# The order of three kinds of subtraction in VectorE's instruction stream, in a hybrid attention and convolution layer

## The reference

```
h    = x * (1 + scale(c)) + shift(c)                 # (2048, 1024), adaLN
proj = h @ w_in + b_in                               # (2048, 1024) @ (1024, 8704)
q, k, v, z_attn, u_x, g_b, g_c, z_conv, g_A, g_B = split(proj)
branch A: dilated sliding-window attention of 12 heads, groups mixed by their softmax denominators,
          (o * silu(z_attn)) @ w_proj_attn
branch B: (g_b * conv3(g_c * u_x) * silu(z_conv)) @ w_proj_conv
x_out = LayerNorm(alpha * x + gate(c) * ((sigmoid(g_A) * y_A + sigmoid(g_B) * y_B) @ w_out + b_out))
```

## Time and profile before

| | us |
|---|---|
| median of 3 runs | 1932.65 |
| lowest and highest | 1930.1, 1934.43 |
| the profiled execution, its time | 1930.85 |
| its span in the profile | 1929.0 |
| TensorE (PE) busy | 1910.6 |
| VectorE (DVE) busy | 1220.3 |
| ScalarE (ACT) busy | 856.1 |

### The profile page before, as it was taken

One profiled execution on the slowest core, in us unless ns is written; L12 is line 12 of the kernel. 1 busy time (PEld: TensorE's weight loads), 2 busy tenths in 40 slices (PEclk: granted clock), 3 DMA queues, 4 the chain that ended last, 5 costly groups with the idle time before them and its releaser, 6 DMA issues.

```text
span 1929.0 us, 25790 instructions
## 1 busy us (share of the span) xinstructions
PE 1910.6 (99%) x9101; PEld 1525.0 (79%) x9101; DVE 1220.3 (63%) x2164; ACT 856.1 (44%) x1506; POOL 199.9 (10%) x354
## 2 busy tenths in 40 slices
PE   8999999999999999999999999999999999999998
PEld 7888888877777777777777777777788888888886
DVE  6755744456666666665686666666656576646776
ACT  3644633344555454666675455544554410012221
POOL 0122111110000000111210000000011100000000
PEclk9999999999999999999999999999999999999999
DMA  9765833342222222364773223323256688884442
GB/s 328 263 204 189 283 99 119 94 112 82 78 83 83 80 79 83 102 206 152 259 265 92 82 83 90 94 86 94 81 150 177 215 242 246 235 269 137 140 144 96
DMA packets 307054, 289.05 MB, mean 150 GB/s; under 512 B 38548, under 2 KB 255760, under 8 KB 304240
## 3 DMA queue, kind: packets, MB, share of 16 engines
q1 hardware_dynamic: 280976, 200.06, 35.6%
q0 software_dynamic: 25952, 87.35, 12.5%
HBM read 198.97 MB, written 88.38 MB: 149 GB/s over the span
## 4 chain that ended last, share of the span: by engine, by line
PE 96%; DVE 2%; issue 1%; ACT 1%; DMA 0%; SPq 0%; DVEq 0%; ACTq 0%
PE acc L1144 22%; PE acc L1149 21%; PE acc L1152 21%; PE acc L1384 3%; PE acc L1319 3%; PE acc L1376 3%; PE acc L1315 3%; PE acc L1380 3%; PE acc L1311 3%; PE score L1221 3%; PE pt_o L1230 2%; PE xb L1253 2%; DVE ada_acc L1708 1%; PE xb L1256 1%; PE xb L1208 1%
## 5 line engine op out<-in xcount | busy, mean ns | idle before, releaser
L1144 PE MATMUL acc<-t_hi,w_hi 128*128 128x512 f32 x1848 | 511.8, 399 | 1.4 <-DVE room L1688 1.3
L1149 PE MATMUL acc<-t_lo,w_hi 128*128 128x512 f32 x1848 | 495.4, 390 | 0.0
L1152 PE MATMUL acc<-t_hi,w_lo 128*128 128x512 f32 x1848 | 495.0, 390 | 0.0
L1144 PEld LDWEIGHTS acc<-t_hi,w_hi 128*128 128x128 f32 x1848 | 336.0, 188 | 89.4 <-issue 20.1
L1149 PEld LDWEIGHTS acc<-t_lo,w_hi 128*128 128x128 f32 x1848 | 346.9, 188 | 74.6
L1152 PEld LDWEIGHTS acc<-t_hi,w_lo 128*128 128x128 f32 x1848 | 346.9, 188 | 74.0
L1688 DVE TENSOR_TENSOR room<-acc,part 128x512 f32<-128x512 f32 x198 | 136.6, 690 | 208.3 <-PE acc L1152 202.9
L1465 ACT ACTIVATE part<-acc,cols 128x512 f32<-128x512 f32 x198 | 136.1, 687 | 217.4 <-PE acc L1152 216.9
L1688 DVE TENSOR_TENSOR room<-room 128x512 f32<-128x512 f32 (+3 forms) x220 | 176.0, 804 | 73.5 <-ACT room L1495 27.4
L1688 DVE TENSOR_TENSOR w_lo<-w_raw,w_hi 128x512 fp32r<-128x512 f32 x272 | 184.2, 685 | 52.0 <-ACT w_hi L1448 51.3
L1448 ACT CAST w_hi<-w_raw 128x512 fp32r<-128x512 f32 x264 | 162.5, 616 | 93.0 <-PE acc L1152 89.7
(11 more groups left out here) (237 smaller groups left out, 2075.8 us busy)
## 6 DMA issues: line engine op xcount, KB each, us to landing
w_raw<-in_w_in SPq DMA_DIRECT2D x132, 512.0 KB, 5.1
gate_d<-room POOLq DMA_DIRECT2D x64, 256.0 KB, 2.8
w_raw<-gate_d SPq DMA_DIRECT2D x32, 512.0 KB, 5.5
qk_d<-room POOLq DMA_DIRECT2D x24, 512.0 KB, 4.2
room<-qk_d SPq DMA_DIRECT2D x192, 64.0 KB, 2.1
room<-in_x SPq DMA_DIRECT2D x32, 256.0 KB, 6.6
t_raw<-tr_d SPq DMA_DIRECT2D x8, 1024.0 KB, 8.4
conv_d<-room POOLq DMA_DIRECT2D x16, 512.0 KB, 2.9
```

The source lines that it names most:

```text
L1144: nc.tensor.matmul(to, w_hi[:, s, k], t_hi[:, p, k], start=(first and k == 0), stop=False, skip_group_check=True)
L1149: nc.tensor.matmul(to, w_hi[:, s, k], t_lo[:, p, k], start=False, stop=False, skip_group_check=True)
L1152: mm = nc.tensor.matmul(to, w_lo[:, s, k], t_hi[:, p, k], start=False, stop=(last and k == KH - 1), skip_group_check=True)
```

## The change

In VectorE's slot loop the block that calls `split_t` moves from behind `split_w` to ahead of `combine`. Nothing is added or removed; in the 14 slots that have a `split_t`, VectorE's order was `combine`, `split_w`, `split_t` and is `split_t`, `combine`, `split_w`.

```diff
                     if m - 2 in ATT_AT[2:]:
                         take_o(ATT_AT.index(m - 2) - 2)
+                    for ph in range(1, 3):
+                        for p in range(NP):
+                            if m == FIRST[ph] + T_LO_AT[p]:
+                                split_t(ph, p)
                     for n, when in enumerate((-4, -3, -2, 0)):
                         if (m - when) % NP == 0 and (m - when) // NP < NG:
                             combine((m - when) // NP, n)
                     if m + 3 < NS:
                         split_w(m + 3)
-                    for ph in range(1, 3):
-                        for p in range(NP):
-                            if m == FIRST[ph] + T_LO_AT[p]:
-                                split_t(ph, p)
```

## The result

The change makes the kernel slower: 1935.82 us (median of 20 runs, 1933.08 to 1938.87) against 1932.42 us (20 runs, 1928.37 to 1934.43). The ratio is 1.0020 with a 95% interval of 1.0013 to 1.0027, which is 3.9 us (2.5 to 5.2) on 1932.42; the two medians lie 3.40 us apart. Beside the experiments the same kernel was run again and gave 1.0031 (1.0019 to 1.0043).

A forecast was written before the change was run, and what follows sets the result against it. TensorE, busy 1910.6 of 1929.0 us, bounds the kernel, with VectorE setting its time at four products. VectorE's 2.80 us plus late loads of 0.95 and 0.4 give 4.15, so 1932.65 + 4.15 = 1936.8 us, range 1933.5 to 1940.0.

The forecast's parts named there:

- Where it counts: TensorE's late starts at products 62, 69, 300, 307: VectorE's sum of p = 4 already sets the time there.
- The four VectorE terms: VectorE, slots before products 62, 69, 300, 307: small subtractions leave a cast wait, delaying the sums 0.70, 0.71, 0.68, 0.71 us.
- SyncE in phase 1: Group 10's weights load 2.9 us later, delaying reloads 3 and 4, their casts and product 69 by 0.95 us.
- SyncE in phase 2: Group 44's late weight load makes reload 3 land at 996.0 instead of 993.1, its cast 0.4 us late.
- The sum: Whole kernel: 0.70 + 0.71 + 0.68 + 0.71 + 0.95 + 0.4 = 4.15 us slower.
- Loads that share the engines: SyncE's queue: weights, reloads 3 and 4 finish together, landing near 232.7 instead of 228.2; +13.6 us, 1946; chance 0.08.
- Hidden loads: Reloads 3 and 4 catch up, so only VectorE's reordering is paid: +2.8 us, 1935.4; chance 0.20.
- Not slower: t_lo of the same product ends the four stalls, so earlier `split_t(ph,6)` shortens them: 1931.0 to 1932.65; chance 0.14.

The follow-up runs named there:

- after_reload_first: Changed kernel, but SyncE issues the weight loads of groups 10 and 44 behind reload 3 of their phase; ratio to the kernel before 1.0010 (1.0001 to 1.0019).
- only_p5: Kernel before with only the `split_t` of reload 5 moved ahead (slots 66 and 304); ratio to the kernel before 1.0015 (1.0005 to 1.0025).
- w_t_combine: Changed kernel with `split_w` ahead of `split_t` again, `combine` still behind it; ratio to the kernel before 1.0000 (0.9991 to 1.0009).
- before_late_w: Kernel before, VectorE's order untouched, SyncE's weight loads of groups 10 and 44 held back for one more `split_w`; ratio 1.0028 (1.0019 to 1.0038).
- only_p1: Kernel before with only the `split_t` of reload 1 moved ahead (slots 59 and 297); ratio to the kernel before 1.0013 (1.0003 to 1.0022).
- after_but_one: Changed kernel with the `split_t` of reloads 3, 4 and 5 of phase 2 in their old place; ratio to the kernel before 1.0012 (1.0004 to 1.0021).
- after_again: The changed kernel run once more, unedited; ratio to the kernel before 1.0031 (1.0019 to 1.0043).
- only_p2_p6: Kernel before with only the `split_t` of reloads 2 and 6 moved ahead; ratio to the kernel before 0.9996 (0.9987 to 1.0005).

## Why the prediction was right, point by point

- *Where it counts.* Right: the four products 62, 69, 300 and 307, each waiting for VectorE's sum of p = 4.
- *The four VectorE terms,* 0.70, 0.71, 0.68, 0.71. Shown: 0.70, 0.70 (0.97 - 0.27, in after_reload_first and only_p5), 0.70, 0.72. The mechanism, small work pushed out of a wait, is shown by w_t_combine, which puts back one subtraction per wait and loses 0.4 us in all.
- *SyncE in phase 1,* 0.95. Right in mechanism (after_reload_first removes it, before_late_w enlarges it). Too large: 0.27 and 0.52 in the two profiles of the changed kernel, and 0.84 (only_p1) and 0.53 (after_but_one) in two more kernels with the late weight load. The step that was off is that a start 2.9 us later pushes every landing out by 2.9. In the profile after, reload 3 landed at 220.66 + 7.7 = 228.4 and reload 4 at 221.9 + 9.7 = 231.6; less the 0.50 us shift that is 2.6 and 2.2 us later than before. So the backlog did catch up, by 0.3 and 0.7 us, and by different amounts in different executions. The stated bounds, 0 to 1.6, hold all four. The prediction also tied this cost to `split_t(1,5)` starting on its cast; only_p1 shows it without that, through reload 4.
- *SyncE in phase 2,* 0.4. Mis-sized: nothing at product 307 in any profile of the changed order. Reload 3 landed at 989.9 + 7.9 = 997.8, which is 2.15 us later than before when the 2.55 us by which TensorE already ran late are taken off, not 2.9; its cast started at 998.19 and didn't wait.
- *The sum.* 4.15 forecast; the stalls grew by 3.1 and 3.3 us. The measured 3.9 (2.5 to 5.2) holds both. That it lies nearer the forecast than the stalls do is in part luck: the load terms were 1.1 and 0.8 us too large in sum, and the next point was missing.
- *What the forecast lacked.* A fall of the granted clock behind product 307. It came in all four profiles whose stall there was 2.0 us (the changed kernel twice, only_p5, after_reload_first) and in none of the nine with 1.56 us or less there, the kernel before among them. It adds about 1.7 us: 3.4 us at half speed. Whether it is part of the timed executions too stays open. By time: with it the changed kernel should be 4.8 to 5.0 us slower, and its two measurements, 3.9 (2.5 to 5.2) and 6.0 (3.7 to 8.3), allow it, the second better than 3.3 without it; after_reload_first should be 4.5 slower and measured 1.9 (0.2 to 3.7), where its stalls alone give 2.8. By clock: one such fall takes 0.0009 off the mean granted clock of an execution. Against the kernel before in the same session this mean was lower by 0.0013 in after_again (6 executions) and by 0.0007 in only_p5 (10), and not lower in after_reload_first (11) or after_but_one (11), with a standard error of 0.0002 to 0.0004 each (the clocks on record have three places). So it seems that most timed executions of the changed kernel have the fall and most of after_reload_first don't, though the one that was profiled has it. The comparison is weak, because the clock also falls in the first 50 us, for anything from 0 to 10.2 us in the thirteen profiled executions.
- *The rivals.* Loads that share the engines (+13.6) did not come: reload 3 landed 7.7 us after its issue, as before (7.5), and products 66 and 67 did not stall. Its price was also added up wrongly, since 10.8 us from 220.5 is 231.3 and not 232.7, and the 4.8 us late became 5.4 in the sum; the case lies far from the measurement either way. Hidden loads (+2.8) are true for phase 2 and not for phase 1. "Not slower" rested on t_lo of product 307 ending the stall; only_p2_p6 moves it 1.2 us earlier and changes nothing.

## What to carry to other kernels

When an engine runs a hand-written order and waits for another engine, the short work placed in front of that wait is free; put a step that is surely going to wait first, and the same work is paid in full wherever the engine has no idle time before its next deadline. Follow the moved work's own semaphores as well: here one late 0.6 us subtraction held back a weight load, behind it on the same queue four reloads, and behind these another engine's casts and sums. To find the better order, look for what stands in front of the operation that TensorE waits for and is needed later than it.

## What the runs showed of the hardware

Idle times of 1.85 to 1.88 us in front of product 307, where TensorE had had no longer idle time for over 990 us, were followed, in four profiles of four, by 3.4 us at 1.2 GHz in the middle of a dense stretch, which began 0.2 to 1.5 us after TensorE resumed. Shorter idle times at these places, up to 1.50 us, were not, in nine profiles of nine. So in this kernel a stall of 2 us can cost nearly twice its length.

That is no threshold for the length of one idle time. At about 41 us every profile has an idle time of 1.32 to 1.37 us, and in 8 of the 13 the clock was at 1.2 GHz for 3.4 us from 1.2 to 2.2 us after it; in the other five it was not. The kernel before is one of the eight:

```profile
41.95 2.00 PE L1101 MATMUL pt_o<-ones,ada_acc 128*128 128x64 f32 x16 [1.32 <-DVE ada_acc L1708]
...
44.00:46.00 2.00, 2.00 (x11) 1.81 (x10) 0.22 (x2) 1.34 (x2) 0.00 (x0) 0.55 0.87 252
46.00:48.00 2.00, 2.00 (x9) 1.55 (x8) 0.68 (x1) 1.26 (x2) 0.00 (x0) 0.60 1.07 280
```

What else decides it, these runs don't show. The Trainium skill (TensorE: Matmul & The Clock Gate, Part 1: The HAM clock gate) says that the default state is the throttled one and that activity releases it. The traces agree in so far as the clock came back to 2.4 GHz during dense matmuls each time; a fall after so short an idle time I had not expected.
